# Three B sets, the scale columns first, and 23 matmuls without a reader in the mixer's front

## What is computed

```python
shift1, scale1, gate1, shift2, scale2, gate2 = jnp.split(c_act @ ada_w[l] + ada_b[l], 6, axis=-1)
h = modulate(rms_norm(x, norm1_g[l]), shift1, scale1)

def s5_mixer(h, lam_re, lam_im, log_dt, b_re, b_im, c_re, c_im, d_skip, w_glu, b_glu):
    dt = jnp.exp(log_dt)[:, None]
    mag = jnp.exp(lr * dt)
    ab_re, ab_im = mag * jnp.cos(li * dt), mag * jnp.sin(li * dt)      # the step of a state
    f_re = (nr * lr + ni * li) / den                                   # nr = ab_re - 1, ni = ab_im
    f_im = (ni * lr - nr * li) / den
    bb_re, bb_im = f * b                                               # complex, 64 groups x 64 states x 16
    ...                                                                # s[t] = ab * s[t-1] + bb @ h[t]
    y = einsum(st_re, cr) - einsum(st_im, ci) + d_skip * h
    g = jax.nn.gelu(y)
    return g * jax.nn.sigmoid(g @ w_glu + b_glu)
```

## Time and profile before

| | |
|---|---|
| median of 3 runs | 1292.57 us (1291.36 to 1295.41) |
| the profiled execution | 1292.06 us, of which the span is 1290.3 |
| PE busy | 1246.6 us, 97% |
| DVE busy | 857.1 us, 66% |
| ACT busy | 604.6 us, 47% |
| POOL busy | 50.2 us, 4% |
| mean granted TensorE clock | 0.984 of full |

### The profile page before, as it was taken

The page is one execution under the profiler, slowest core; times in us unless marked ns, Lnnn a source line. Parts: engine busy times, 40 slices in busy tenths (PEclk is TensorE's granted clock), DMA queues, the critical chain, the costliest instruction groups (busy, mean ns, idle before and its releaser), DMA issues.

```text
span 1290.3 us, 25331 instructions
## 1 busy us (share of the span) xinstructions
PE 1246.6 (97%) x10936; PEld 1164.3 (90%) x10936; DVE 857.1 (66%) x1173; ACT 604.6 (47%) x781; POOL 50.2 (4%) x67
## 2 busy tenths in 40 slices
PE   5989999999999999999999999999999999999997
PEld 4667899999966489999999999999998999999997
DVE  6999678886537776768456655447459666666443
ACT  5845633433335565543445434336334545544342
POOL 5300000000000000000000000000000000000000
PEclk8969999999999999999999999999999999999998
DMA  9965478987652928655565554455455434655452
GB/s 262 315 217 174 163 258 299 326 293 256 209 180 96 295 86 278 217 173 165 165 208 177 178 180 147 156 186 161 134 164 160 135 131 131 202 189 194 143 177 74
DMA packets 219705, 247.03 MB, mean 191 GB/s; under 512 B 5872, under 2 KB 209088, under 8 KB 219616
## 3 DMA queue, kind: packets, MB, share of 16 engines
q1 hardware_dynamic: 211616, 218.63, 52.2%
q0 software_dynamic: 7648, 26.86, 6.1%
q10 hardware_dynamic: 352, 0.23, 0.1%
HBM read 244.66 MB, written 1.05 MB: 190 GB/s over the span
## 4 chain that ended last, share of the span: by engine, by line
PE 87%; DVE 7%; ACT 2%; DMA 2%; issue 1%; ACTq 0%; DVEq 0%
PE PS L1746 86%; ACT PARTS L592 1%; DVE ARENA L1154 1%; DMA RING<-in_ada_w 0%; DMA H<-in_s_log_dt 0%; DMA RING<-in_mla_w_uq 0%; DVE X L1158 0%; DMA RING<-in_w_in 0%; DVE ARENA L1262 0%; DVE PARTS L1012 0%; PE PS L2375 0%; DVE ARENA L1324 0%; DVE WL L1034 0%; DVE ARENA L1265 0%; DVE SQ L995 0%
## 5 line engine op out<-in xcount | busy, mean ns | idle before, releaser
L1746 PE MATMUL PS<-PARTS 128*128 128x256 f32 (+3 forms) x3608 | 839.8, 283 | 0.0
L1746 PEld LDWEIGHTS PS<-PARTS 128*128 128x128 f32 (+1 forms) x3608 | 619.3, 189 | 1.4 <-issue 0.9
L1034 DVE TENSOR_TENSOR WL<-RING,PARTS 128x2048 fp32r<-128x2048 f32 (+2 forms) x189 | 387.3, 2053 | 236.3 <-ACT PARTS L592 236.1
L1746 PE MATMUL PS<-HH,WL 128*128 128x256 f32 (+3 forms) x1832 | 520.9, 284 | 1.9 <-DVE PARTS L1003 0.9
L1746 PE MATMUL PS<-HH,PARTS 128*128 128x256 f32 (+3 forms) x1832 | 518.6, 283 | 0.0
L592 ACT CAST PARTS<-RING 128x2048 fp32r<-128x2048 f32 (+2 forms) x189 | 324.0, 1716 | 290.9 <-DMA RING<-in_w_ffn_out 66.8
L1746 PEld LDWEIGHTS PS<-HH,WL 128*128 128x128 f32 (+1 forms) x1832 | 345.1, 188 | 7.8 <-issue 4.9
L1746 PEld LDWEIGHTS PS<-HH,PARTS 128*128 128x128 f32 (+1 forms) x1832 | 344.4, 188 | 0.4
L1746 PE MATMUL PS<-PARTS,WL 128*128 128x256 f32 (+1 forms) x832 | 236.9, 285 | 0.8 <-DVE PARTS L1645 0.5
L1746 PEld LDWEIGHTS PS<-PARTS,WL 128*128 128x128 f32 x832 | 158.1, 190 | 2.7 <-issue 1.8
L1746 PE MATMUL PS<-ARENA 128*32 128x63 f32 (+8 forms) x864 | 59.2, 272 | 4.3 <-issue 3.1
(11 more groups left out here) (348 smaller groups left out, 992.8 us busy)
## 6 DMA issues: line engine op xcount, KB each, us to landing
RING<-in_w_ffn_in SPq DMA_DIRECT2D x44, 1024.0 KB, 5.1
RING<-in_ada_w SPq DMA_DIRECT2D x32, 1024.0 KB, 8.6
RING<-in_ffn_w_gate SPq DMA_DIRECT2D x22, 1024.0 KB, 5.3
RING<-in_ffn_w_up SPq DMA_DIRECT2D x22, 1024.0 KB, 5.2
RING<-in_w_in SPq DMA_DIRECT2D x20, 1024.0 KB, 5.2
ARENA<-in_ada_w POOLq DMA_DIRECT2D x16, 1024.0 KB, 7.3
RING<-in_ffn_w_down SPq DMA_DIRECT2D x16, 768.0 KB, 4.5
RING<-in_w_ffn_out SPq DMA_DIRECT2D x16, 768.0 KB, 4.2
```

Of the source, the lines that this page charges most:

```text
L1034: V.tensor_tensor(WL[:, u % SLOTS, 0:w], RING[:, u % SLOTS, 0:w], WH[:, u % SLOTS, 0:w].bitcast(fp32), SUB)\
L1746: return nc.tensor.matmul(o, lhsT, rhs, start=start, stop=stop)
```

## The change

Five things are changed, all in front of the GLU.

- The small operations: `log_dt` is loaded first, ACT takes its Exp broadcast over states, PE turns three rows (`lam_re`, `lam_im`, `dt`) and everything else is done at 128x32 in `LT`. f is multiplied into `WPOW` by a shorter chain.
- Three B sets: set 0 is `BRAW` itself, so `BD` serves both `bt_of(0)` and `taps`; sets 1 to 3 use the powers 1 to 3, and each has a block buffer of its own. `CT4` stands one power higher against B, so `taps` makes three distances, D comes in `y_of` as a product of its own (`SKIP`), without the identity matmuls, and `CT4[0]` reads the state of its own chunk.
- The angles are sums of eight coarse and eight fine steps; `c_set` has a buffer for each set; `c_set` 0 to 2 stand ahead of `turned_in`.
- Scale columns first (`ADA_ORDER`); the stream's order, the place of the late constants, and the order of `stat(0)`, `std(0)`, `ada_rows`, `bt_of`, `b_blocks`, `row_copy` on PE and ACT. `ada_rows(4)` goes behind the first four `b_u`, `ada_rows(6)` behind the last, `ada_rows(8)` behind `taps`, `ada_rows(9)` behind `y_of(1)`. The head of `y_of` no longer waits for `s_done`.
- `keep_warm` seven times, 23 matmuls in all.

```diff
+ADA_ORDER = (2, 3, 0, 1, 4, 5, 6, 7, 8, 9)
...
+        BDK = [None] + [arena(a, 2 * PAIRS * 32)[0] for a in (KW_AT, KW_AT + 2 * KT * P, LAYER_AT)]
+        CSET_LATE, _ = arena(KW_AT + 2 * KT * P, 4, PAIRS, GCH)
...
+        CSET_EARLY, _ = arena(at, 4, PAIRS, GCH)
+        TURNS, _ = arena(at, 8, PAIRS * 8)
...
+        AT["ada_front"] = len(UNITS)
+        for _s in ADA_ORDER:
+            UNITS.extend((ADA0[:, :, _c:_c + 256], KT, 256) for _c in (_s * 512, _s * 512 + 256))
...
+                if u == 8:
...
+            act.dma_start(LROW[0:PAIRS, 3, 0:2], A["s5_log_dt"][0].rearrange("(k two) -> k two", two=2)).then_inc(S["s5_loaded"], 16)
             act.dma_start(LROW[0:PAIRS, 0, :], A["s5_lam_re"][0].rearrange("(k two) n -> k (two n)", two=2)).then_inc(S["s5_loaded"], 16)
             act.dma_start(LROW[0:PAIRS, 1, :], A["s5_lam_im"][0].rearrange("(k two) n -> k (two n)", two=2)).then_inc(S["s5_loaded"], 16)
...
+            act.wait_ge(S["s5_loaded"], 48)
+            nc.scalar.activation(LROW[0:PAIRS, 2, :].rearrange("p (g n) -> p g n", g=2),
+                                 LROW[0:PAIRS, 3, 0:2].unsqueeze(2).broadcast_to([PAIRS, 2, NST]), ACT.Exp).then_inc(S["lrow_act"], 1)
...
+            act.wait_ge(S["lrow_dve"], 1)
+            nc.scalar.activation(LAM[:, 0, :], LT[:, 3, :], ACT.Exp).then_inc(S["lrow_act"], 1)
+            nc.scalar.preload_act_table_set("trig_and_small")
+            for b in range(2):
+                act.wait_ge(S["xt_ready"], b + 1)
+                nc.scalar.copy(X[:, 2 * b:2 * b + 2, NMETA:], PS[:, b, :].rearrange("p (m t) -> p m t", m=2)).then_inc(S["res_ready"], 2)
+            act.wait_ge(S["lrow_dve"], 2)
+            nc.scalar.activation(LT[:, 13, :], LT[:, 6, :], ACT.Sin).then_inc(S["lrow_act"], 1)
+            nc.scalar.activation(LT[:, 14, :], LT[:, 7, :], ACT.Sin, scale=-1.0, bias=hpi).then_inc(S["lrow_act"], 1)
...
-            act.wait_ge(S["s5_loaded"], 48)
...
+            for b in range(2, 4):
+                act.wait_ge(S["xt_ready"], b + 1)
+                nc.scalar.copy(X[:, 2 * b:2 * b + 2, NMETA:], PS[:, b, :].rearrange("p (m t) -> p m t", m=2)).then_inc(S["res_ready"], 2)
+            squares(0)
...
-            for b in range(4):
-                act.wait_ge(S["xt_ready"], b + 1)
-                nc.scalar.copy(X[:, 2 * b:2 * b + 2, NMETA:], PS[:, b, :].rearrange("p (m t) -> p m t", m=2)).then_inc(S["res_ready"], 2)
-            squares(0)
...
-                if k is None:
+                if k == 0:
                     act.wait_ge(S["b_loaded"], 32)
-                elif k >= 2:
-                    act.wait_ge(S["bt_ready"], 2 * k - 2)
+                    act.wait_ge(S["norm_stat"], 1)
                 for i in range(2):
-                    if k is not None:
-                        act.wait_ge(S["b_pow"], 2 * k + i + 1)
-                    src = (BRAW if k is None else BPOW[:, 2 * (k % 2):2 * (k % 2) + 2, :, :])[:, i, :, :]
-                    dst = BD[:, i, :, :] if k is None else BDK[:, k % 2, :].rearrange("p (i k c) -> p i k c", i=2, c=32)[:, i, :, :]
+                    if k == 0:
+                        src, dst = BRAW[:, i, :, :], BD[:, i, :, :]
+                    else:
+                        act.wait_ge(S["b_pow"], 2 * k + i - 1)
+                        src, dst = BPOW[:, 2 * (k % 2) + i, :, :], BDK[k].rearrange("p (i k c) -> p i k c", i=2, c=32)[:, i, :, :]
                     for g in range(2):
                         ins = nc.scalar.activation(dst[:, :, g * GCH:(g + 1) * GCH], src, ACT.Copy, scale=half[g])
-                ins.then_inc(S["bd_zero" if k is None else "bd_exp"], 1)
...
+            std(0)
+            b_blocks(0)
+            meta_copy()
+            b_blocks(1)
             c_compact()
-            b_blocks(0)
             row_copy(0)
-            std(0)
-            b_blocks(1)
-            nc.scalar.preload_act_table_set("trig_and_small")
-            row_copy(1)
             bt_out(0)
             b_blocks(2)
+            row_copy(1)
+            nc.scalar.preload_act_table_set("trig_and_small")
+            b_blocks(3)
+            bt_out(1)
             row_copy(2)
-            bt_out(1)
-            b_blocks(3)
-            row_copy(3)
             bt_out(2)
             bt_out(3)
+            row_copy(3)
+            act.wait_ge(S["ada_used"], 1)
             shift(0, ADA_SHIFT1)
-            b_blocks(None)
             act.wait_ge(S["turn_cos"], 1)
             nc.scalar.activation(by_pair(SIN), by_pair(SIN), ACT.Sin, scale=2 * PI_IN)
             nc.scalar.activation(by_pair(COS), by_pair(COS), ACT.Sin, scale=-TWO_PI, bias=hpi).then_inc(S["turn_sin"], 1)
             c_blocks(0)
             c_blocks(1)
-            c_blocks(2)
+            act.wait_ge(S["ct_exp"], 2)
             nc.scalar.activation(RMUL[:, :, 1:], R4[:, 0, :].unsqueeze(2).broadcast_to([P, PAIRS, NCH - 1]), ACT.Copy)
             nc.scalar.activation(RMUL[:, :, 0:1], R4[:, 0, :].unsqueeze(2), ACT.Copy, scale=0.0).then_inc(S["r_ready"], 1)
+            c_blocks(2)
             c_blocks(3)
             k_out()
             act.wait_ge(S["bu_ready"], KT)
...
+            dve.wait_ge(S["lam_ready"], 1)
+            V.tensor_copy(LT[:, 0:3, :], PS[:, 6, 0:3 * PAIRS].rearrange("p (r k) -> p r k", k=PAIRS)).then_inc(S["lam_used"], 1)
+            dve.wait_ge(S["lam_used"], 1)
+            V.tensor_tensor(L[3], L[0], L[2], MUL).then_inc(S["lrow_dve"], 1)
+            link(V.tensor_tensor(L[4], L[1], L[2], MUL))
...
+            dve.wait_ge(S["lrow_act"], 4)
+            V.tensor_tensor(power(0, 0), LAM[:, 0, :], L[14], MUL)
+            V.tensor_tensor(R4[:, 1, :], LAM[:, 0, :], LAM[:, 0, :], MUL)
+            link(V.tensor_tensor(power(1, 0), LAM[:, 0, :], L[13], MUL))
+
...
+                dst = BPOW[:, 2 * (k % 2):2 * (k % 2) + 2, :, :]
+                if k >= 2:
+                    dve.wait_ge(S["b_pow"], 2 * k - 2)
+                V.tensor_tensor(BTMP[:, :, :, :], by_channel(POW, 1, k - 1), BRAW[:, :, :, :], MUL)
+                if k == 3:
+                    dve.wait_ge(S["bd_exp"], 2)
+                link(V.tensor_tensor(dst, by_channel(POW, 0, k - 1), BRAW[:, :, :, :], MUL))
+                V.tensor_tensor(dst[:, 0, :, :], dst[:, 0, :, :], BTMP[:, 1, :, :], SUB).then_inc(S["b_pow"], 1)
+                V.tensor_tensor(dst[:, 1, :, :], dst[:, 1, :, :], BTMP[:, 0, :, :], ADD).then_inc(S["b_pow"], 1)
+
...
+            V.tensor_scalar(L[15], power(0, 0), 1.0, None, SUB)
+            V.tensor_tensor(L[17], power(1, 0), L[1], MUL)
...
+            link(times(POW, 1, 1, POW, (power(0, 0), power(1, 0)), 2))
...
-            for k in range(CHUNK):
-                dst = BPOW[:, 2 * (k % 2):2 * (k % 2) + 2, :, :]
+            for k in range(1, CHUNK):
+                b_set(k)
...
+            for g, steps_of in enumerate((coarse, fine)):
+                V.tensor_tensor(part[3 * g], steps_of, turn, MUL)
+                V.tensor_tensor(part[3 * g + 1], steps_of, low_part, MUL)
+                ins = V.tensor_tensor(part[3 * g + 2], steps_of, high_part, MUL)
+            link(ins)
+            link(V.tensor_scalar(TURNS[:, 0:4:3, :], TURNS[:, 0:4:3, :], MAGIC, MAGIC, ADD, SUB))
+            link(V.tensor_tensor(TURNS[:, 2:6:3, :], TURNS[:, 2:6:3, :], TURNS[:, 0:4:3, :], SUB))
+            link(V.tensor_tensor(TURNS[:, 2:6:3, :], TURNS[:, 2:6:3, :], TURNS[:, 1:5:3, :], ADD))
+            by_step = f.rearrange("p k (a b) -> p k a b", b=8)
+            link(V.tensor_tensor(by_step, part[2].unsqueeze(3).broadcast_to([P, PAIRS, 8, 8]),
+                                 part[5].unsqueeze(2).broadcast_to([P, PAIRS, 8, 8]), ADD))
+            link(V.tensor_scalar(m, f, MAGIC, MAGIC, ADD, SUB))
+            link(V.tensor_tensor(f, f, m, SUB))
+            V.tensor_scalar(m.bitcast(i32), f.bitcast(i32), 0x7FFFFFFF, None, ALU.bitwise_and).then_inc(S["turn_cos"], 1)
...
+                a = CSETS[k]
+                t = CIM[:, :, :, :]
...
-            m, f = by_pair(COS), by_pair(SIN)
-            turn, high_part, low_part = (LAM[:, r, :].unsqueeze(2).broadcast_to([P, PAIRS, NCH]) for r in (1, 2, 3))
-            V.tensor_tensor(RMUL[:, :, :], T_CH, low_part, MUL)
-            link(V.tensor_tensor(m, T_CH, turn, MUL))
-            link(V.tensor_scalar(m, m, MAGIC, MAGIC, ADD, SUB))
-
-            link(V.tensor_tensor(f, T_CH, high_part, MUL))
-            link(V.tensor_tensor(f, f, m, SUB))
-            link(V.tensor_tensor(f, f, RMUL[:, :, :], ADD))
-            link(V.tensor_scalar(f, f, 0.5, -0.5, ALU.min, ALU.max))
+                    dve.wait_ge(S["c_pow"], k)
...
             dve.wait_ge(S["tr_ready"], 1)
-            dve.wait_ge(S["late_loaded"], 16)
             V.tensor_copy(VEC[:, :], PS[:, 6, 0:SEQ]).then_inc(S["tr_used"], 1)
             dve.wait_ge(S["tr_used"], 1)
+            dve.wait_ge(S["ada_cols"], 2)
+            modulation(8, 16, PS[:, 5, 8:16])
+            link(gain(0, ADA_SCALE1, VAT["norm1_g"]))
+            rstd(0)
```

(84 more changed lines are left out.)

163 lines of the change are left out of this document (61 added, 102 removed).

## The result

The changed kernel takes 1299.76 us in the median (1298.86 to 1303.45), the kernel before 1292.57 (five runs, 1288.62 to 1295.41); the ratio is 1.0062, 95% interval 1.0039 to 1.0085: 0.6% slower, where 0.5% faster was forecast. The profiled execution took 1299.76 us, its span is 1298.0. The first GLU matmul is at 124.81 us; it was at 121.01 and forecast at 114.4.

The account below looks back on a forecast made before the run. PE's dense work from the first GLU matmul (121.01 us) was taken to bound the end. Terms before it sum to 6.65 us gained (GLU at 114.4), carried one for one: 1292.57 - 6.65 = 1285.9 us, range 1281.5 to 1290.5.

Parts of the forecast that it names:

- The start, the B sets, the angles: DVE's work before `b_u`: angles done at 41.0 instead of 50.5, but only 0.65 us reach the first `b_u`.
- `taps`: Before `y_of`: eight groups without identity matmuls fall from 6.7 to 4.1 us, +2.6 gained.
- `y_of` etc. on both sides: 0: In `y_of`: same columns, `ada_rows(9)` and two gaps near 1.5 us before and after, so no difference.
- `b_u(4..7)` at full clock: +6.2: Second half of `b_u`: 7.72 us instead of 13.93, 6.2 us gained.
- 16 x 0.43: From `b_u(3)` to `taps`: sixteen readerless matmuls at 0.43 us each cost 6.9 us.
- wrong if the clock falls once between 50 and 90: From `b_u` on: one fall of the granted clock at 50 to 90 us would refute the forecast.
- The weight stream: -0.7: At `ada_rows(8)`: the stream idles some 5 us, unit 17 lands 0.7 us late.
- The 10.8 us of the earlier trace: Late-weights rival: first unit lands after 10.8 us, `ada_rows(8)` waits 5 to 6 us more, 1291.4 us; chance 0.08.
- `ada_rows(4)` moves: -1.9: From before `b_u`, where it was free, to behind the first `b_u` matmuls: 1.9 us lost.
- The clock rival: Slower rival: PE at half clock when the first `b_u` starts, price 11.4 us, 1297.3 us; chance 0.06.
- The rule on transposes: Skill's rule that transposes do not raise the clock: PE would be slow from `bt_of(2)` on; given a small chance.
- No chance of its own: Rival that the clock stays up without readerless matmuls: they are only their price, already in the sum; no chance given.

Follow-up runs that it names:

- e1: Changed kernel without any of its 23 readerless matmuls: 1293.71 us, ratio 1.0002 to the kernel before.
- e2: Changed kernel without the 16 readerless matmuls behind `b_u(3)`, the 7 ahead of `b_u` kept: 1296.15 us, ratio 1.0020.
- e3: Changed kernel with `ada_rows(4)` back in front of `b_u(0)`, all 23 readerless matmuls kept: 1291.99 us, ratio 1.0001.
- e13: The changed kernel measured again, nothing altered: 1299.44 us, ratio 1.0044 to the kernel before.
- e14: Changed kernel with the ada row steps in the order from before the change, all 23 readerless matmuls kept: 1292.66 us, ratio 0.9980.
- e11: e7 without the seven readerless matmuls in front of `b_u`, so none of the 23 is left: 1290.75 us, ratio 0.9983.
- e7: Changed kernel with ada row steps in their order from before the change and without the 16 readerless matmuls behind `b_u(3)`: 1286.36 us, ratio 0.9937.
- e6: Changed kernel with the last three GLU weight units held until `y_of(4)` is done: 1303.01 us, ratio 1.0071.
- e4: Changed kernel with `ada_rows(4)` back in front of `b_u(0)` and none of the 23 readerless matmuls: 1300.38 us, ratio 1.0047.
- e15: e7 with `ada_rows(6)` alone left behind `b_u(7)`: 1294.18 us, ratio 1.0016.

## Why the prediction was wrong, point by point

**The start, the B sets, the angles: right.** First B product at 16.45 us (17.1 forecast), angles ended at 39.2 (41.0), H scaled by 43.4 (45.3), and the first `b_u` at 50.52 (52.4), with DVE waiting 2.64 us for the ada columns as forecast. The stall in the third B set did not come, the sets ended at 27.6; the angles then took 11.7 us, not 10.9. The bitwise absolute value took 1.23 us, the value taken. This part was 1.9 us better than forecast. `turned_in` ran at 60.2 to 65.1 and DVE's last state was there at 106.5, as forecast. `taps` took 2.82 us in all, not 4.1: another 1.3.

**"`y_of` etc. on both sides: 0" failed: 3.8 us.** The two idle times near 1.5 us were seen in the trace of before and booked as equal on both sides without asking what they are. They are not a property of `y_of` but of instruction 256n + 193 meeting the weight stream. Before they sum to 3.06 us from `b_u` on, after to 6.93, 3.87 of it in `y_of`. Half clock cost 2.5 us behind it, in `y_of(4)` and a part of `y_of(5)`, and 0.6 in `y_of(0)` behind the wait for `RING`.

**"`b_u(4..7)` at full clock: +6.2" and "16 x 0.43" failed by what lay between: 7.5 us.** The mechanism was right (`b_u(4..7)`'s matmuls ran at 7.47 us for 246), but `b_u(0..3)` took 9.5 us instead of 7.7 and `b_u(4..7)` 10.0 instead of 7.7, through the idle times of 1.21 and 1.85 us and half clock behind. The readerless and ada matmuls behind the two halves took 8.7 and 9.0 us instead of 7.2 each, since the clock fell there in spite of them: the first group of four (eight records) took 3.22 and 2.96 us, where a group at full clock takes 1.99. The forecast's condition "wrong if the clock falls once between 50 and 90" was met twice.

**"The weight stream: -0.7" had the landing right and missed what hangs on it: 2.3 us.** Units 16 and 17 were issued when `ada_rows(6)` was done and landed after 5.2 and 7.8 us (forecast 5.1 and 8.1; lines of the changed kernel, 84 to 86 us, by source):

```profile
L441 SPq DMA_DIRECT2D RING<-in_ada_w x2: 368/475/582, 84.3 to 84.7; - x2
DMA to landing us min/median/max: 5.2/6.5/7.8
```

So `ada_rows(8)` began 8.3 us behind the end of `ada_rows(6)`, and the forecast had 8.4 (1.7 + 1.9 + 4.1 + 0.7). The 10.8 us of the earlier trace rows, given 0.08 as a rival, did not come. The wait was 1.97 us instead of 0.7 because `taps` was done 1.3 earlier: that gain was returned in it. And `ada_rows(8)` ran at half clock behind the wait, 2.96 us instead of 1.90. In the ten traces with `ada_rows(6)` behind `b_u(7)` the distance from its end to `ada_rows(8)` is 8.2 to 9.7 us, however little stands between them (e1 waited 5.38 us, e2 5.17). So nothing saved between the two can be paid out, while the chain above runs through `ada_rows(6)`, and a us saved before it counts.

**"`ada_rows(4)` moves: -1.9" was too small.** The move was priced at 2.3 us in all (-1.9, +0.3, -0.7). Taken back alone (e3) it measures 5.6 to 7.9, and with the places of the other two as well 6.8 (e13, e14). What the forecast left out is that `ada_rows(4)`, wide matmuls in front of `b_u`, stood where the clock is decided: behind it `b_u(0..3)` kept full clock in ten traces of ten, without it in two of six.

**The clock rival had a price and too small a chance.** Half clock in the first `b_u` (0.06) was absent from the first trace but there in four of six traces of the same instructions. The rule on transposes did not decide it: the clock was full at 48 to 50 us after the transposes, then fell or not.

**"No chance of its own" for the readerless matmuls was wrong both ways.** The seven in front of `b_u` are worth 4 to 6 us (e11), taking out the 16 behind gains 5.6 (e14 against e7), of which the shift of the idle times is a part. The forecast had the first as 1.3 us of cost on the path.

From the forecast GLU at 114.4 to 124.8: -1.9 (start), -1.3 (`taps`), +7.5 (from `b_u` to `taps`), +2.3 (the wait for `RING` and `ada_rows(8)` at half clock), +3.8 (`y_of`) = +10.4. Three of these terms are one omission: the forecast let PE run through 50 to 121 us at full clock without an idle time; three idle times put down to issue, the wait for `RING` and half clock took it. The 3.9 us of the tail were not foreseen and are not shown to belong to the change.

## What to carry to other kernels

An idle time that the profile puts down to nothing is a term of its own: find what it is periodic in before booking it as equal on both sides; here it stands only at each 256th instruction, in runs of narrow matmuls while weights stream. When weights pass through a ring of few slots, the step that frees a slot sets the date of the load some slots later: follow that date through the new order first, since everything saved between that step and the resulting wait is returned in it. Matmuls without a reader paid in front of a real wait that would have dropped the clock (e11); where useful matmuls could stand in the same place, the kernel was faster without them (e7 against e14).

## What the runs showed of the hardware

- TensorE's program comes in packets of 16 KB, one for 256 instructions. In runs of narrow matmuls, while weights stream (235 to 360 GB/s in the five microseconds before), it can come late: 44 idle times of 0.9 to 3.9 us, always at 256n + 193 instructions, each ended 2.3 to 2.7 us after a packet had started. With the stream off (5 GB/s, e6) there was none.
- The clock fell during 27 of these 44 or within 2.2 us behind them; in three it was half already, in 14 it stayed full. In `b_u`, matmuls of 32 rows did not bring it back: 13.93 us for 256 in e4, 7.73 for 138 in e7. Whether it fell in the first `b_u` differed between executions of the same instructions.
- Two 1 MB units issued together after a pause of the stream landed after 5.1 to 5.2 and 7.7 to 7.8 us (the changed kernel and e15).
